# Attention of a two-layer hybrid block on one core: transposes and values one step earlier, a reciprocal per head, and one batch of idle products less

## The reference, cut to what matters

```python
s = jnp.einsum('bqkgd,bskd->bkgqs', q, k).astype(F32) * (q.shape[-1] ** -0.5)
p = jax.nn.softmax(s, axis=-1)          # group B adds one sink logit per head
o = jnp.einsum('bkgqs,bskd->bqkgd', p.astype(v.dtype), v)
```

## Time and profile before

| | us |
|---|---|
| median of 3 runs | 1706.0 |
| lowest and highest | 1705.37, 1706.23 |
| profiled execution | 1705.96 |
| its span | 1704.2 |
| PE busy | 1628.7, 96% of the span |
| attention of layer 0, first scores to first product by `g_mat` | 202.57 to 322.75 |
| attention of layer 1, the same | 1160.40 to 1242.49 |

### The profile page before, as it was taken

One profiled execution on the slowest core, in us unless ns is written; L12 is line 12 of the kernel. 1 busy time (PEld: TensorE's weight loads), 2 busy tenths in 40 slices (PEclk: granted clock), 3 DMA queues, 4 the chain that ended last, 5 costly groups with the idle time before them and its releaser, 6 DMA issues. The chain is left out here.

```text
span 1704.2 us, 23677 instructions
## 1 busy us (share of the span) xinstructions
PE 1628.7 (96%) x9500; PEld 1386.0 (81%) x9500; DVE 819.5 (48%) x1240; ACT 448.8 (26%) x937; POOL 860.1 (50%) x844
## 2 busy tenths in 40 slices
PE   6999999999899999999999999999999999999997
PEld 4777866768899997899998778786778988788885
DVE  5354254447673415444454684635557421520058
ACT  5511365433500011100002164125534200210021
POOL 4444034543464444544445571532576577677772
PEclk9999999999999999999999999999999999999999
DMA  9211033322343212243642120210023452233321
GB/s 363 77 50 54 22 108 119 104 80 62 100 142 118 91 64 68 65 146 113 209 161 77 57 86 25 74 50 8 14 64 97 141 149 93 93 99 99 99 87 50
DMA packets 157004, 160.93 MB, mean 94 GB/s; under 512 B 6376, under 2 KB 111960, under 8 KB 156896
## 3 DMA queue, kind: packets, MB, share of 16 engines
q1 hardware_dynamic: 136560, 121.40, 23.3%
q10 hardware_dynamic: 20336, 38.03, 6.8%
HBM read 157.31 MB, written 2.10 MB: 94 GB/s over the span
## 5 line engine op out<-in xcount | busy, mean ns | idle before, releaser
L682 POOL TENSOR_SCALAR ring_hi<-stage 128x512 fp32r<-128x512 f32 x352 | 248.4, 706 | 595.8 <-PE ps L758 569.3
L685 POOL TENSOR_TENSOR ring_lo<-stage,ring_hi 128x512 fp32r<-128x512 f32 x352 | 491.4, 1396 | 29.4
L756 PE MATMUL ps<-act_hi,ring_hi 128*128 128x384 f32 (+2 forms) x1088 | 379.6, 349 | 0.0
L758 PE MATMUL ps<-act_hi,ring_lo 128*128 128x384 f32 (+2 forms) x1088 | 378.0, 347 | 0.0
L757 PE MATMUL ps<-act_lo,ring_hi 128*128 128x384 f32 (+2 forms) x1088 | 377.9, 347 | 0.0
L756 PE MATMUL ps<-ring_hi,act_hi 128*128 128x512 f32 (+1 forms) x700 | 280.4, 401 | 11.2 <-DVE act_lo L1863 5.0
L758 PE MATMUL ps<-ring_hi,act_lo 128*128 128x512 f32 (+1 forms) x700 | 272.4, 389 | 0.0
L757 PE MATMUL ps<-ring_lo,act_hi 128*128 128x512 f32 (+1 forms) x700 | 272.3, 389 | 0.0
L758 PEld LDWEIGHTS ps<-act_hi,ring_lo 128*128 128x128 f32 x1088 | 204.6, 188 | 13.3
L757 PEld LDWEIGHTS ps<-act_lo,ring_hi 128*128 128x128 f32 x1088 | 204.7, 188 | 12.9
L756 PEld LDWEIGHTS ps<-act_hi,ring_hi 128*128 128x128 f32 x1088 | 204.6, 188 | 12.9
(11 more groups left out here) (267 smaller groups left out, 2147.8 us busy)
## 6 DMA issues: line engine op xcount, KB each, us to landing
stage<-in_w_gate_up_dram SPq DMA_DIRECT2D x88, 512.0 KB, 5.0
mod_stage<-in_w_mod_dram ACTq DMA_DIRECT2D x56, 512.0 KB, 4.3
stage<-in_w_in_dram SPq DMA_DIRECT2D x18, 1024.0 KB, 5.1
stage<-in_w_down_dram SPq DMA_DIRECT2D x16, 1024.0 KB, 5.0
stage<-in_w_mod_dram SPq DMA_DIRECT2D x12, 1024.0 KB, 5.3
start_mod<-in_w_mod_dram SPq DMA_DIRECT2D x8, 1024.0 KB, 11.2
stage<-in_w_down_dram SPq DMA_DIRECT2D x8, 768.0 KB, 4.4
stage<-in_w_out_dram SPq DMA_DIRECT2D x16, 256.0 KB, 4.5
```

The costliest lines, as they stand in the source:

```text
L682: nc.gpsimd.tensor_scalar(hi_, stage[:, par, j * 512:(j + 1) * 512], 1.0, 0.0, ALU.mult, ALU.add).then_inc(w_hi, 1)
L685: nc.gpsimd.tensor_tensor(lo_, stage[:, par, j * 512:(j + 1) * 512], hi_.bitcast(F32), ALU.subtract).then_inc(w_ready, 1)
L756: nc.tensor.matmul(o, a_hi, b_hi, start=first, stop=False)
L758: return nc.tensor.matmul(o, a_lo, b_hi, start=False, stop=last)
```

## The change

Transposes and values move one step closer to the scores: in step s PE now issues scores of s, transposes of s-1 and values of s-2. Where s is a context pair, or s = n, the order within the step is values first and transposes last (`late`). The n+3 steps become n+2. ACT issues the exponentials first, then `out_hi` of s-2, then all of `read_T` of s-1. DVE issues the maxima of s, a reciprocal per head of s, `read_T` of s-1, the portion of `inner_decay`, and `out_low` of s-2. POOL waits for each head's reciprocal by itself. The 18 idle products of layer 0 go; the 28 of layer 1 become 20 and move from the start of step 2 to step 1, behind the scores of pair 1.

```diff
--- before.py
+++ after.py
@@ -540,7 +540,7 @@
                 "qk_read": sum(blocks), "ssq_ready": NT, "squares": NT, "rms_sd": NT, "qkw_in": 32 if l == 0 else 48, "qkw_set": 1, "sink_set": 1,
                 "scores_a_ready": n_attn, "scores_b_ready": n_attn, "neg_ready": 2 * n_attn, "probs_ready": 2 * n_attn,
                 "probs_T_done": chunks_to(l, n_attn), "probs_T_act": chunks_to(l, n_attn, (0, 2)),
-                "probs_T_dve": chunks_to(l, n_attn, (1,)), "den_ready": n_attn, "values_done": n_attn, "scaled": 2 * n_attn,
+                "probs_T_dve": chunks_to(l, n_attn, (1,)), "den_ready": 2 * n_attn, "values_done": n_attn, "scaled": 2 * n_attn,
                 "o_hi": n_attn, "o_lo": n_attn, "sink_in": 16, "pos_in": 16, "zeta_ready": 1, "v_decayed": NT,
                 "state_sums": 1, "state_set": 1, "xi_ready": 1, "q_decayed": 4, "inner_arg": 1, "inner_exp": 1, "inner_set": 1, "mix_zero": 1, "four_sums": 2, "mix_in": 80, "dft_in": 16, "four_copied": 3 if need_ctx else 2, "four_ready": 1,
                 "g_done": 1, "g_ready": 1, "ab_done": nt, "ab_ready": nt, "four_done": 4 if need_ctx else 2,
@@ -688,9 +688,9 @@
             def attention(l):
 
                 for i, (g, t, b, keys) in enumerate(attn_pairs(l)):
-                    need(pool, "den_ready", l, i + 1)
                     n = len(keys) * P
                     for a in range(2):
+                        need(pool, "den_ready", l, 2 * i + a + 1)
                         m = 2 * (i % 2) + a
                         nc.gpsimd.tensor_scalar(probs_slot(2 * i + a)[:, 0:n], probs_slot(2 * i + a)[:, 0:n], rden[:, m:m + 1], 0.0,
                                                 ALU.mult, ALU.add).then_inc(sem("scaled"), 1)
@@ -1018,10 +1018,7 @@
                     mm.then_inc(sem("values_done"), 1)
 
                 columns = attn_columns(l)
-                for s in range(total + 3):
-                    if s == 2 and l == DEPTH - 1:
-                        need(pe, "probs_ready", l, 1)
-                        keep_clock(5, 28)
+                for s in range(total + 2):
                     if 1 < s <= total:
                         need(pe, "probs_ready", l, 2 * s)
                     if s == 1:
@@ -1033,15 +1030,19 @@
                         scores(s)
                     if s == 1 and l < DEPTH - 1:
                         keep_clock(6, 28)
-                    if 2 <= s < total + 2:
-                        transpose_probs(s - 2)
-                    if s == 2 and l < DEPTH - 1:
-                        keep_clock(6, 18)
+                    if s == 1 and l == DEPTH - 1:
+                        need(pe, "probs_ready", l, 1)
+                        keep_clock(5, 20)
+                    late = s == total or 1 <= s < total and len(pairs[s][3]) == CT
+                    if 1 <= s < total and not late:
+                        transpose_probs(s - 1)
+                    if s >= 2:
+                        values(s - 2)
                     if s == total:
                         channel_mix(l)
                         key_values(l)
-                    if s >= 3:
-                        values(s - 3)
+                    if late:
+                        transpose_probs(s - 1)
 
             def key_values(l):
 
@@ -1542,7 +1543,7 @@
                     need(act, "neg_ready", l, 2 * i + a_head + 1)
                     if a_head == 0:
                         if i >= 2:
-                            need(act, "den_ready", l, i - 1)
+                            need(act, "den_ready", l, 2 * (i - 1))
                         if i >= 3:
                             need(act, "probs_T_done", l, chunks_to(l, i - 2))
                     elif i >= 2:
@@ -1594,20 +1595,20 @@
                         a.activation(chunk_decay[:, :], lg_half[:, l, :, :].rearrange("p d c -> p (d c)"), ACT.Exp,
                                      scale=float(P)).then_inc(sem("zeta_ready"), 1)
 
-                for s in range(total + 3):
+                for s in range(total + 2):
                     loads(s)
                     if s == total // 2 + 4:
                         need(act, "values_done", l, total // 2)
                         act.dma_start(dft[:, :, :], tab["dft"]).then_inc(sem("dft_in"), 16)
-                    if 2 <= s < total + 2:
-                        read_T(s - 2, 0)
                     if s < total:
                         probabilities(s, 0)
                         probabilities(s, 1)
-                    if 2 <= s < total + 2 and chunks(pairs[s - 2]) > 2:
-                        read_T(s - 2, 2)
-                    if s >= 3:
-                        out_hi(s - 3)
+                    if s >= 2:
+                        out_hi(s - 2)
+                    if 1 <= s <= total:
+                        read_T(s - 1, 0)
+                        if chunks(pairs[s - 1]) > 2:
+                            read_T(s - 1, 2)
                     if s == 10:
                         need(act, "inner_arg", l, 1)
                         a.activation(inner[:, :, :], inner[:, :, :], ACT.Exp).then_inc(sem("inner_exp"), 1)
@@ -2099,12 +2100,12 @@
                         need(dve, "values_done", l, i - 1)
                     v.tensor_copy(probs_T[i % 2][:, 4 * P:(4 + n) * P], ps[:, 5, 0:n * P]).then_inc(sem("probs_T_dve"), 1)
 
-                def denominators(i):
-                    m = slice(2 * (i % 2), 2 * (i % 2) + 2)
-                    need(dve, "probs_ready", l, 2 * i + 2)
+                def denominator(i, a):
+                    m = 2 * (i % 2) + a
+                    need(dve, "probs_ready", l, 2 * i + a + 1)
                     if i >= 2:
-                        need(dve, "scaled", l, 2 * (i - 1))
-                    v.reciprocal(rden[:, m], expsum[:, m]).then_inc(sem("den_ready"), 1)
+                        need(dve, "scaled", l, 2 * (i - 2) + a + 1)
+                    v.reciprocal(rden[:, m:m + 1], expsum[:, m:m + 1]).then_inc(sem("den_ready"), 1)
 
                 def out_low(i):
                     g, t, b, _ = pairs[i]
@@ -2115,22 +2116,22 @@
                 dve.wait_ge(ring_used, win_last_slot(l, 4) + 1)
                 done(v.memset(mix_bd[:, :, :], 0.0), "mix_zero")
                 columns = attn_columns(l)
-                for s in range(total + 3):
+                for s in range(total + 2):
                     if s in columns:
                         if s < total:
                             need(dve, "scores_a_ready", l, s + 1)
                         read_columns(columns[s], 1, 488)
-                    if 1 <= s < total + 1:
-                        denominators(s - 1)
                     if s < total:
                         maximum(s, 0)
                         maximum(s, 1)
-                    if 2 <= s < total + 2 and chunks(pairs[s - 2]) > 1:
-                        read_T(s - 2)
-                    if s >= 3:
-                        out_low(s - 3)
+                        denominator(s, 0)
+                        denominator(s, 1)
+                    if 1 <= s <= total and chunks(pairs[s - 1]) > 1:
+                        read_T(s - 1)
                     if s in (7, 8, 12):
                         inner_decay(l, s)
+                    if s >= 2:
+                        out_low(s - 2)
                     if s == total + 1:
                         scan(l)
```

## The result

| | before | changed |
|---|---|---|
| median of 15 runs each, us | 1704.74 | 1707.48 |
| lowest to highest | 1702.68 to 1707.51 | 1706.05 to 1711.77 |
| mean granted clock over the runs (before: its 96 runs beside the experiments) | 0.9917 | 0.9920 |
| scores of pair 2 to `retention_scores`, layer 0 | 117.47 | 122.62 |
| the same, layer 1 | 77.88 | 77.88 |

The ratio is 1.0021, 95% interval 1.0013 to 1.003: 0.2% slower (3.6 us), where a gain of 1.4 us was forecast. The two profiled executions have spans of 1704.2 and 1707.1 us. Layer 0's stretch is 5.15 us longer, layer 1's the same; the remaining -2.2 us lies in the other stages and goes with the low clock, which falls in other places in each run (before twice as long at 20 to 40 us and again at 440, 1010 to 1030 and 1080 to 1100, changed for longer at 1310 to 1330).

The account below looks back on a forecast made before the run. PE, busy 96% of the span, was taken as the bound, taking turns with the exponentials' loop in layer 0's attention. Gains of 0.65 (layer 0) and 2.1 - 1.35 (layer 1) sum to 1.4 us: 1704.6 from 1706.0, range 1701.0 to 1708.6.

Parts of the forecast that it names:

- Layer 0 step by step: Layer 0's attention, step lengths summed from the scores of pair 2: 111.1 us, before 112.7.
- V: End of the last values in a layer's attention; forecast 1.6 us earlier in layer 0, 2.1 in layer 1.
- Idle products: Removing layer 0's 18 takes 2.1 us off PE, since other work now stands there; layer 1's start worth 0.
- Start of the exponentials: ACT in layer 1: exponentials ahead of `read_T` gain 0.13 per five-key, 0.27 per four-key, 0.03 per A step; sum 1.0 us.
- signs of being wrong: Layer 0 context steps without stall, shorter layer 1 A step, low clock around the tails, differences outside the two attention stretches.
- the last exponential to V: End of layer 1's attention: outputs, values, `channel_mix`, `key_values`, transposes, copy and last values take 8.4 us.
- The tail: Behind the last values, `g_mat` and `scan` now come later: loss 0.95 us in layer 0, 1.35 in layer 1.
- The rival that the tail is free: `g_mat`, `xi`, `scan` covered behind the last pair: gain 3.7 us, 1702.3; chance 0.22 together with short stalls.
- s = 9: Layer 0: values of pair 7 wait for `out_low` behind the decay table's second portion (1.13 us); 1.5 us stall.
- s = 3: Layer 0 context step: values of pair 1 wait 0.9 us for `out_hi` and two `read_T`; step 4.49 us.
- s = 24 and 25: The last two steps of layer 0's attention, forecast at 7.7 us together.
- The clock rival (slower): Waits at tails and layer 0 stalls drop PE to 1.2 GHz three times more: 3.7 us slower, 1709.7; chance 0.15.

Follow-up runs that it names:

- e3: The kernel before without its 18 idle products in layer 0; median 1706.14 us, ratio 1.001 to the kernel before.
- e10: The changed kernel with the 18 idle products put back behind the scores of pair 2 in layer 0; 1711.29 us, ratio 1.0042 to before.
- e6: The kernel before with only the two exponentials of a step moved ahead of the first `read_T` on ACT; 1703.35 us, ratio 0.9987 to before.
- e5: The changed kernel with the decay portions between DVE's maxima and reciprocals; 1707.86 us, ratio 1.0011 to the kernel before.
- e2: The changed kernel with `g_mat`, `xi` and `scan` again ahead of the last pair's output copies; 1707.97 us, ratio 1.0015 to the kernel before.
- e11: The changed kernel with transposes ahead of values in the context steps too; 1708.08 us, ratio 1.0009 to the kernel before.
- e7: The changed kernel with layer 0 in the old order, with its 18 idle products; 1703.31 us, ratio 0.9988 to the kernel before.
- e8: Layer 0 old order, exponentials first; layer 1 new order, decay table behind `out_low`, `g_mat`, `xi`, `scan` before the last outputs; 1704.42 us, 0.9996 to before.
- e9: Layer 0 old order, exponentials first; layer 1 new order, `g_mat`, `xi`, `scan` before last outputs; both, decay between maxima and reciprocals; 1699.80 us, 0.9975 to before.
- e12: The changed kernel with 15 idle products in the stall of step 9 of layer 0; 1709.28 us, ratio 1.003 to the kernel before.

## Why the prediction was wrong

It forecast 1704.6 with 0.63 on "within 0.2%"; 1707.48 lies in its range, but the difference is 0.2% to the other side. **The step that failed is "Layer 0 step by step"**: its sum of 111.1 us from the scores of pair 2 to V. Measured were 116.9, or 114.0 at full clock. Point by point:

- **Idle products: right as far as PE's order goes.** In the old order their removal moved nothing (e3), in the new one it is worth the 2.1 us (e10). What they do to the clock, which the forecast put at nothing, stays open (e3).
- **Start of the exponentials: right in sign and place.** B steps gain 0.20 each (forecast 0.13 with five keys, 0.27 with four), A steps 0.09 (forecast 0.03); e6 shows the cause. A shorter A step was even one of its signs of being wrong. In layer 1 the gain up to the last exponential, 0.9 for the forecast 1.0, is luck: the steps themselves gave 1.9 and not 1.15, and steps 8 and 9 took 9.70 us against 8.75 before, where I allowed 0.1, which is the collision again, since in e5 they take 8.38. From the last exponential to V it took 9.03 us and not 8.4, as `values` of 14 waited 1.42; so the gain ahead of V was 1.4, not 2.1.
- **The tail: right**, 0.93 in layer 0 and 1.44 in layer 1 for the forecast 0.95 and 1.35, and e2 takes both back. The rival that the tail is free falls with it.
- **s = 9: the mechanism right, its size wrong.** The 1.13 us of the earlier trace rows was measured while POOL waited for a reciprocal. The change issues the reciprocals ahead of the portion, so POOL runs beside it: 2.18 us. The step at s = 9 took 6.94 us at full clock and not 6.07, and, through L2158's 1.40 instead of 0.88, that at s = 8 4.97 and not 4.60: +1.2 together. e5 shows it from the other side: with POOL idle the two steps take 10.21 us.
- **Waits left out of the walk.** At s = 3 `values` wait 1.20 us, forecast 0.9 (+0.3: 4.82 against 4.49). At s = 16 and 22 the steps come out 0.3 and 0.25 longer: I had `fill_rows` cover the wait for the output, but that is in front of it. At s = 19 `values` wait 0.91 us, forecast 0.65, and the step is 0.36 longer. From s = 23 to V it took 12.4 us and not 11.5: at s = 24 `fill_rows` wait 1.21 us, and the last `values` 0.98 for `act_lo`, as they did before the change; which of them the forecast's 7.7 for s = 24 and 25 left out it doesn't say. Together +2.1; e11 shows that 2.0 us of the context steps' length (1.3 of it at s = 9) is the choice of values first. The other steps, a little shorter than forecast, give back 0.5.
- **The clock rival (slower): low clocks fell at its places, but no more of them.** Of the eight profiled kernels with the new order in layer 0 four have an episode at s = 6, three at s = 9 and four at s = 18; of the seven with the longer wait behind V in layer 1 three have one within 1.4 us of V (e7, e10, e11), of the seven others none. But the old order has its own, four times of six at s = 18: in layer 0's attention the traces show 5.5 us at the low clock per kernel with the new order and 5.1 with the old one. Over 15 runs the mean clock did not fall (0.9920 to 0.9917), and at equal clock the loss is still 3.6 us. In the profiled run alone it accounts for 2.2 of the 5.15 us.

Two slips of its sums change nothing: the terms from the last exponential to V add up to 8.3 and not 8.4, and two episodes at its own price of 1.7 us would end at 1708.0, not at 1706.6.

At full clock the account reads: layer 0 ahead of V +2.0, tails +2.4, layer 1 ahead of V -1.4, sum +3.0; forecast -1.6, +2.3 and -2.1, sum -1.4. Of the 4.4 us between them 3.7 are in layer 0: 2.9 by which the walk was short, and 0.8 since its 112.7 us for before held an episode of low clock.

Rows of before could have warned of the collision: there POOL's scaling starts just behind the reciprocal, and the reciprocal is what the change moves. What stays open: the 0.6 us between the profile's 3.0 and the 3.6 at equal clock, within the error of the fit; and what decides how many episodes a kernel meets (e8).

## What to carry to other kernels

A duration read from a trace holds for what ran beside it: before moving an instruction of DVE, look at what POOL does at its new place, and put filler work where POOL waits for DVE. When a pipeline is made one step shorter, write down for each engine what now stands ahead of the release that the next stage waits for, at the irregular steps and in the last two above all, for there the step's slack is gone. And try the parts of a reordering singly: here one moved copy on ACT held the gain of the steady steps, and the loss of 3.7 us went with layer 0's order, where the places of the decay table (e5), of the tail (e2) and of the context transposes (e11) each cost some of it. The new order in layer 0 with all three mended was not run; by the step lengths I estimate 116.4 us for its stretch (119.7 less 1.7, 0.9 and 0.7), against 114.8 in e9.

## What the runs showed of the hardware

- Four fp32 `SCALAR_TENSOR_TENSOR` of 128x128 on DVE take 1.13 us with POOL idle and 1.98 to 2.19 beside POOL's fp32 work. POOL's durations hardly change where it started first (0.90 to 0.92 a scaling, `v_decay` 1.07 against 1.04), but `v_decay` takes 1.47 where DVE's `inner<-inner,ident_r` (L2166) was under way.
- Idle products that keep the clock up in one stall do not lessen the low clock of the run: added to the changed kernel the mean clock was 0.9916 (e12) and 0.9910 (e10), without them 0.9920. In e12's profile the episode stood at s = 18 and no longer at s = 9. Taken away from the kernel before (e3) it was 0.9906 against 0.9917, which may be theirs or the scatter between kernels.
- A kernel in which PE is busy for 95% of the span still spends some 10 us a run (6.5 to 17) of PE's work on the low clock, in three to eight pieces of mostly 1.7 us or twice that, and about 70% of it arrives at the end (1.19 us per 0.001 of the mean clock, which is 1.7 us of work).
